# State-space mixer: the next state's weighed rows ahead of the present state's sums, and one mask product for each bank of decays

## The reference, cut to what matters

```python
acum = jnp.cumsum(dtc * a.reshape(g, hg), axis=2)
seg = acum[:, :, :, None] - acum[:, :, None, :]
decay = jnp.where(lower, jnp.exp(jnp.where(lower, seg, 0.0)), 0.0)
cb = jnp.einsum('bctgn,bcsgn->bctsg', cc, bc)
y_diag = jnp.einsum('bctsg,bctsgh,bcsghp->bctghp', cb, decay, xdt)
decay_end = jnp.exp(acum[:, :, -1:] - acum)
states = jnp.einsum('bcsgn,bcsgh,bcsghp->bcghpn', bc, decay_end, xdt)
chunk_decay = jnp.exp(acum[:, :, -1])
# scan over the chunks: h = chunk_decay * h + states, h_prev is h ahead of the chunk
y_off = jnp.einsum('bctgn,bctgh,bcghpn->bctghp', cc, jnp.exp(acum), h_prev)
y = y_diag + y_off
```

## Time and profile before

| | |
|---|---|
| median of 3 runs | 3119.91 us (3112.3 to 3123.27) |
| the profiled execution | 3118.5 us, its span 3117.0 us |
| busy: TensorE (PE) | 2496.0 us, 80% |
| busy: VectorE (DVE) | 1209.9 us, 39% |
| busy: ScalarE (ACT) | 895.8 us, 29% |
| busy: GpSimd (POOL) | 108.0 us, 3% |
| HBM traffic | 262 GB/s over the span |
| mean granted TensorE clock | 0.915 of full speed |

### The profile page before, as it was taken

One profiled execution on the slowest core, in us unless ns is written; L12 is line 12 of the kernel. 1 busy time (PEld: TensorE's weight loads), 2 busy tenths in 40 slices (PEclk: granted clock), 3 DMA queues, 4 the chain that ended last, 5 costly groups with the idle time before them and its releaser, 6 DMA issues.

```text
span 3117.0 us, 30294 instructions
## 1 busy us (share of the span) xinstructions
PE 2496.0 (80%) x12349; PEld 1432.3 (46%) x12349; DVE 1209.9 (39%) x2046; ACT 895.8 (29%) x1408; POOL 108.0 (3%) x177
## 2 busy tenths in 40 slices
PE   6975687599999995997687777589688997777686
PEld 4734565478888884543222222144384443222222
DVE  2367547489999994163200000132471012000001
ACT  3334313278888874042000000032031002000000
POOL 1010300100000001000000000000000000000000
PEclk9986788799999997998799999889789998999998
DMA  9393630289999995283799999842003434999997
GB/s 337 126 368 131 214 127 2 108 325 390 393 396 393 393 366 191 75 323 136 275 401 398 402 402 402 312 156 72 23 5 105 147 126 166 409 409 409 409 409 282
DMA packets 246853, 819.45 MB, mean 263 GB/s; under 512 B 11075, under 2 KB 11241, under 8 KB 246448
## 3 DMA queue, kind: packets, MB, share of 16 engines
q1 hardware_dynamic: 226688, 753.88, 62.7%
q0 software_dynamic: 14432, 45.54, 4.3%
q10 hardware_dynamic: 5584, 17.98, 1.5%
HBM read 779.46 MB, written 37.90 MB: 262 GB/s over the span
## 4 chain that ended last, share of the span: by engine, by line
PE 58%; DMA 25%; DVE 10%; ACT 3%; issue 2%; SPq 1%; POOL 0%; DVEq 0%; PEldq 0%; ACTq 0%; POOLq 0%
PE PS L245 55%; DMA ring<-in_moe_w_up 8%; DMA ring<-in_w_e_up 6%; DMA ring<-in_w_e_down 3%; DMA ring<-in_moe_w_gate 2%; DMA ring<-in_w_e_gate 2%; DMA ring<-in_ada_w 1%; PE PS L1803 1%; SPq L375 1%; DMA ring<-in_moe_w_down 1%; DVE hgrn L949 1%; PE PS L551 1%; DVE SM L2415 0%; DMA row<-YP,DST 0%; DMA SM<-in_router_w 0%
## 5 line engine op out<-in xcount | busy, mean ns | idle before, releaser
L411 DVE TENSOR_TENSOR cut<-ring,cut 128x1024 fp32r<-128x1024 f32 x424 | 501.9, 1222 | 179.7 <-ACT cut L403 168.6
L403 ACT CAST cut<-ring 128x1024 fp32r<-128x1024 f32 x424 | 438.2, 1054 | 264.6 <-PE PS L245 239.0
L245 PE MATMUL PS<-cut,xeT 128*128 128x512 f32 x1536 | 364.7, 394 | 3.0 <-DVE cut L411 3.0
L245 PEld LDWEIGHTS PS<-cut,xeT 128*128 128x128 f32 x1536 | 285.9, 189 | 67.4 <-DVE cut L411 5.9
L245 PE MATMUL PS<-ring,hidT 128*64 128x512 f32 (+1 forms) x1024 | 242.7, 624 | 74.2 <-DMA ring<-in_w_e_down 37.9
L245 PE MATMUL PS<-ring,xeT 128*64 128x512 f32 x1024 | 239.2, 614 | 69.4 <-DMA ring<-in_moe_w_up 35.4
L245 PE MATMUL PS<-ring,XE 128*32 128x512 f32 x1008 | 230.5, 608 | 68.9 <-DMA ring<-in_w_e_up 44.6
L245 PE MATMUL PS<-HT,ring 128*128 128x512 f32 (+2 forms) x576 | 206.4, 526 | 1.2 <-DVE HT L524 1.2
L245 PE MATMUL PS<-cut,hidT 128*128 128x512 f32 x768 | 179.6, 393 | 4.5 <-DVE hidT L1812 4.5
L245 PEld LDWEIGHTS PS<-ring,xeT 128*64 128x64 f32 x1024 | 77.0, 140 | 230.2 <-issue 170.3
L245 PEld LDWEIGHTS PS<-ring,hidT 128*64 128x64 f32 (+1 forms) x1024 | 71.9, 128 | 231.8 <-issue 176.1
(11 more groups left out here) (534 smaller groups left out, 2552.0 us busy)
## 6 DMA issues: line engine op xcount, KB each, us to landing
ring<-in_moe_w_gate SPq DMA_DIRECT2D x64, 2048.0 KB, 14.0
ring<-in_moe_w_up SPq DMA_DIRECT2D x64, 2048.0 KB, 13.2
ring<-in_moe_w_down SPq DMA_DIRECT2D x64, 2048.0 KB, 13.6
ring<-in_w_e_up SPq DMA_DIRECT2D x32, 2048.0 KB, 18.5
ring<-in_w_e_down SPq DMA_DIRECT2D x32, 2048.0 KB, 20.6
ring<-in_w_e_gate SPq DMA_DIRECT2D x31, 2048.0 KB, 18.4
ring<-in_ada_w SPq DMA_DIRECT2D x24, 2048.0 KB, 15.1
ring<-in_w_in SPq DMA_DIRECT2D x13, 2048.0 KB, 7.7
```

The costliest lines, as they stand in the source:

```text
L245: return pe.matmul(o, l, r, start=start, stop=stop, **kw)
L403: act.copy(self.bufs[i % len(self.bufs)][0], w).then_inc(self.high.sem, 1)
L411: dve.tensor_tensor(low, w, high.bitcast(F32), ALU.subtract).then_inc(self.low.sem, 1)
```

## The change

1. The weighing becomes a function `weigh(n)`. The first two are issued ahead of the first operation; weighing n + 2 is issued behind the sums of the "to" operation that used weighing n. Six are issued in all, into the same two buffers by turns, as before.
2. The second use of a "from" operation writes its four weighed groups into four parts of a buffer of 128 x 1536 (`shares`, which is the second `XWs`, free by then), waits once, and adds them to `Y2` in a single instruction of 1536 columns. Eight instructions and seven waits become five and one.
3. In `decays`, one product of the identity with both masks (repeated twice, 512 columns) opens the bank; the four products with `DA` accumulate onto it. Eight products a bank become five.

```diff
+    shares = XWs[1]
...
     def states_vector():
-        n, made_by = 0, []
+        into = [k for k, op in enumerate(STATES) if op[0] == "to"]
+
+        def weigh(n):
+
+            if n >= len(into):
+                return
+            _, d, c, _ = STATES[into[n]]
+            if n > 1:
+                dve.wait_ge(*op_made(into[n - 2]))
+            dve.tensor_tensor(heads(XWs[n % 2]), heads(XH[:, c, :]),
+                              WS[:, c * 48 + d * 24:c * 48 + d * 24 + 24].unsqueeze(2).to_broadcast([P, 24, 64]),
+                              ALU.mult).then_inc(weighted.sem, 1)
+
+        weigh(0)
+        weigh(1)
         for k, (way, d, c, first) in enumerate(STATES):
             b = bank(4 * (k % 2), 4)
+            if k:
+                dve.wait_ge(*op_taken(k - 1))
+            dve.wait_ge(*op_made(k))
             if way == "to":
-                if n > 1:
-                    dve.wait_ge(*op_made(made_by[n - 2]))
-                dve.tensor_tensor(heads(XWs[n % 2]), heads(XH[:, c, :]),
-                                  WS[:, c * 48 + d * 24:c * 48 + d * 24 + 24].unsqueeze(2).to_broadcast([P, 24, 64]),
-                                  ALU.mult).then_inc(weighted.sem, 1)
-                made_by.append(k)
-                n += 1
-                if k > 1:
-                    dve.wait_ge(*op_taken(k - 1))
-                dve.wait_ge(*op_made(k))
                 for g in range(4):
...
             else:
-                dve.wait_ge(*op_taken(k - 1))
-                dve.wait_ge(*op_made(k))
-                t = spare[:, 0:384]
                 for g in range(4):
-                    y = Y2[:, c, g * 384:(g + 1) * 384]
+                    y, t = Y2[:, c, g * 384:(g + 1) * 384], shares[:, g * 384:(g + 1) * 384]
                     if first:
                         ins = dve.tensor_tensor(heads(y), heads(b[:, g * 512:g * 512 + 384]), by_head(EA, c, d, g), ALU.mult)
                     else:
-                        vs.settle(dve.tensor_tensor(heads(t), heads(b[:, g * 512:g * 512 + 384]), by_head(EA, c, d, g), ALU.mult))
-                        ins = dve.tensor_tensor(y, y, t, ALU.add)
-                        if g < 3:
-                            vs.settle(ins)
+                        vs.add(dve.tensor_tensor(heads(t), heads(b[:, g * 512:g * 512 + 384]), by_head(EA, c, d, g), ALU.mult))
+                if not first:
+                    dve.wait_ge(*vs.now)
+                    ins = dve.tensor_tensor(Y2[:, c, :], Y2[:, c, :], shares, ALU.add)
             ins.then_inc(op_taken.sem, 1)
+            if way == "to":
+                weigh(into.index(k) + 2)
...
+            mm(two(bank(v % 3)), ident, KC[:, C_NF:C_NF + 2 * P].unsqueeze(1).to_broadcast([P, 2, 2 * P]), True, False)
             for hh in range(2):
                 for d in range(2):
                     o = bank(v % 3)[:, (hh * 2 + d) * P:(hh * 2 + d + 1) * P]
                     col = c * 48 + d * 24 + 2 * u + hh
-                    mm(o, DA[:, col:col + 1].to_broadcast([P, P]), KC[:, (C_LE, C_GE)[d]:(C_LE, C_GE)[d] + P], True, False)
-                    last = mm(o, ident, KC[:, (C_NF, C_NB)[d]:(C_NF, C_NB)[d] + P], False, True)
+                    last = mm(o, DA[:, col:col + 1].to_broadcast([P, P]), KC[:, (C_LE, C_GE)[d]:(C_LE, C_GE)[d] + P], False, hh + d == 2)
```

## The result

| | before | after |
|---|---|---|
| median | 3117.74 us (4 runs, 3112.3 to 3123.27) | 3085.23 us (4 runs, 3081.36 to 3092.2) |
| profiled execution, its span | 3118.5 us, 3117.0 us | 3081.36 us, 3079.9 us |
| mean granted TensorE clock | 0.915 | 0.913 |

The ratio of after to before is 0.9905, with a 95% interval of 0.9889 to 0.9922, some 30 us (24 to 35). A second measurement of the same two kernels, five rounds, gave 0.9909 (0.9896 to 0.9923).

The account below looks back on a forecast made before the run. It took the states stage as bound by VectorE and TensorE handing over, the within stage by TensorE: 3118.5 - 29.5 - 0.8 = 3088.2 us, plus half of 1.4, gives 3089 us; own range 3082 to 3095, with the lower clock 3080 to 3101.

Parts of the forecast that it names:

- three signs of being wrong: VectorE's states-stage waits over 8 us, a 512-column pass over 0.5 us, or the chain's loads starting at the same time.
- What bounds the stages: States stage: VectorE and TensorE hand over, each busy about 42 of 76.6 us; within stage: TensorE bounds it.
- rival of an absorbed gain: Behind the two stages, a load doesn't start earlier and the gain is lost: about 3118 us, chance 5%.
- Part 1 with part 2: States stage with weighings forward and single additions: 47.2 us in place of 76.66, a gain of 29.5 us.
- best case: States stage at its shortest: 46.2 us, a gain of 30.5 us.
- wait of 0.6: States stage: VectorE's wait for TensorE's second group, taken as 0.6 us, between 0 and 1.8.
- allowance for a fallen clock: States stage: 0.6 us added, a bit over a quarter of about 2 us lost if TensorE's clock falls.
- gap of 2.7 us: States stage: TensorE's gap ahead of operation 5; a clock fall there costs VectorE about 2 us before operations 5 and 6.
- worst case: States stage with TensorE at its lower clock throughout: 59.7 us, a gain of 17.0 us.
- rival of a nearly free product: Within stage: the wide mask product costs almost nothing, TensorE drops to VectorE's pace: 3073 us, chance 2%.
- rival of a slow product: Within stage: the mask product's repeated operand is slow, at four times the price 2.6 us more a bank: 3151 us, chance 4%.
- rival of the lower clock: States stage: TensorE stays at its lower clock and bounds it, 59.7 us: 3100.7 us in all, chance 7%.

Follow-up runs that it names:

- e1: The kernel before with only the weighings moved forward, old second "from" sums and old mask products: 3089.24 us, ratio 0.9912, states stage 48.72 us.
- e5: The changed kernel with the 512-column mask product made twice in each bank: both within stretches 83.44 us, 20.61 more.
- changed once more: The changed kernel unaltered, measured again on the same chip as e9: 3088.44 us, ratio 0.9909, states stage 44.89 us.
- e6: The changed kernel with weighings 2 to 5 moved from VectorE to GpSimd: states stage 48.90 us, 4 us more.
- e7: The changed kernel with the two first copies of the states on ScalarE instead of VectorE: states stage 44.44 us, 0.5 us less.
- e4: The kernel before, order unchanged, with identity products filling five of TensorE's gaps in the states stage: that stage 64.94 us, 11.7 less.
- e2: The kernel before with only the new second "from" sums, one addition of 1536 columns: states stage 74.70 us, 1.96 less.
- e8: The changed kernel with identity products in TensorE's gaps ahead of the states stage and at its end: 3081.48 us, ratio 0.9881.
- e9: The changed kernel with e8's fillers, e7's copies on ScalarE and more fillers behind operation 4 and late in each within stretch: 3077.62 us, ratio 0.9878.

## Why the prediction was right

The time forecast was 3089 us, and 3085.23 and 3088.44 us were measured; the gain was 30.3 us by the sum and about 30 by the ratio. That it came so near is in part luck: the profiles, which tell the stages to within a us or two, have 31.7 us in the states stage for 29.5 forecast and 1.2 to 1.6 in the within stage for 0.8, so the sum was about 3 us too small, and the scatter of the first part and of the ratio (24 to 35 us) hides it. None of the three signs of being wrong came: VectorE's waits are 3.9 us, not more than 8, a pass of 512 columns takes 0.43 us, and the loads start earlier. Point by point:

- **What bounds the stages.** Confirmed. e1 shows the gain of a mere change of VectorE's order in the states stage, e5 that TensorE has no slack in the within stage.
- **Nothing is lost behind.** Confirmed to 0.1 us between the two profiles, 779.6 to 782.8 us over all runs. The rival of an absorbed gain is out.
- **Part 1 with part 2: 47.2 us forecast, 44.94 measured.** That is below the 46.2 us given as the best case, which the terms don't give either: 46.6 less the wait of 0.6 is 46.0. VectorE's own 41.0 us were measured as 40.6. The rest of the difference is mostly three waits that were taken too large: the first (3.9 us by the sum) is 2.88, as the clock rose inside the first group; the second (0.6) is none; the allowance for a fallen clock (0.6) wasn't needed. The wait ahead of operation 6 is 1.03 for 0.9. The first wait took one of two values in the six profiles that start the stage so: 2.88, 2.83 and 2.81 us (changed, e5, changed once more) and 3.98, 3.98 and 3.97 (e1, e6, e7), and the sum took the upper one as certain. A fall in the gap of 2.7 us costs 0.8 us on VectorE (e1), where I had priced it at 2: the wait ahead of operation 6 exists anyway and shrinks when operation 5 comes late.
- **The clock's share** was in the sum without being named as a price. It is 11.7 of the 31.7 us in the old order (e4). An engineer who had counted on the new order at the old clock would have forecast 17.0, the prediction's own worst case, which is an estimate.
- **Part 2: 1.9 us on the path.** Measured 1.96 (e2).
- **Part 3: 0.8 us, 2.20 us a pair.** The pair is 2.20 us and the average of the profiles says 1.2 us. The rival of a nearly free product is out: after the change, too, a pass of 512 columns takes 0.43 us. The Trainium skill, TensorE: Matmul & The Clock Gate, in its part on the back-to-back issue gap, has 131 ns for one product of 512 columns in a stream and 81 ns for one of 128; these float32 passes don't agree, with 0.43 and 0.11 us. The rival of a slow product is out (e5: 0.86 us with the repeated operand, the price of the earlier trace rows). The Trainium skill, PSUM — Partial Sum Buffer, in its specifications, says that any non-contiguous access slows matmuls significantly; if it means a moving operand that repeats two neighbouring blocks, this measurement doesn't agree.
- **The rival of the lower clock** did not come in the changed kernel: there, in e1, e5, e7, e8 and e9 TensorE was at its higher level from the third group on, but for operation 5 in e1 and e8. Of the runs with the new order only e6, behind a gap of 6.50 us, had it at the lower one for longer.

## What to carry to other kernels

When two engines are each busy for half of a stage, ask of every instruction in front of a wait whether it needs what the wait brings; a preparation for step n + 1 belongs ahead of the sums of step n. Price the shorter gaps by the clock as well: here the higher clock alone was worth 11.7 of 31.7 us, by TensorE no longer falling to its lower level in gaps of 3.7 to 5.9 us. And before work is moved to an idle engine, look at which memory both engines read: ScalarE's copies from PSUM left VectorE's instructions at their usual lengths (e7), GpSimd's products from SBUF did not (e6).

## What the runs showed of the hardware that was not expected

- Beside GpSimd's products in SBUF, two of VectorE's instructions with both inputs in SBUF took 3.15 and 3.11 us in place of 0.54, until the end of the GpSimd product beside each; the copies, which read PSUM, were not slower (e6, four instructions of one kind, in one profile).
- Identity products into columns of banks that nothing reads kept TensorE at its higher clock in gaps of 3.7 to 5.9 us, at almost no cost to the useful ones (e4: the stage is 11.7 us shorter, where the five shorter groups alone make 11.4). Of the 8.8 us that e9's profile is ahead of the changed kernel's in the last three columns of the table, 2.8 lie in the states stage, partly by the copies on ScalarE, 3.9 in the within stage and 2.1 behind, where e1 without fillers is 1.7 ahead as well.
- The same gap of 2.68 us let the clock fall in e1 and e8 and not in e5, e7 and the two profiles of the changed kernel.
